# Values ahead of keys in the second layer's projections, samples' values from the same weights, and another spread of the projection units over the steps

## The reference

```python
def shared_kv(x, c, w_ada_kv, b_ada_kv, w_kv):
    sh, sc = jnp.split(c @ w_ada_kv + b_ada_kv, 2, axis=-1)
    kv = modulate(x, sh, sc) @ w_kv          # 1024 -> 1024 key columns, then 1024 value columns
    return kv[..., :KW_B].reshape(...), kv[..., KW_B:].reshape(...)
...
q = (xm @ w_q_b[lb]).reshape(n, t, H_B, 2 * DH_B) * (DH_B ** -0.5)
if prompt:
    o = diff_attn_prompt(q, k_sh, v_sh, lam)               # 512 x 512 scores, 8 heads x 2 maps
else:                                                      # 8 samples x 16 cached pages of 128 rows, and the own new row
    o = diff_attn_sample(q, k_sh, v_sh, cache_k, cache_v, page_table, lam)
```

## Time and profile before

| what | value |
|---|---|
| median of 3 runs | 1865.09 us (1860.26 to 1868.95) |
| the profiled execution's own time | 1866.28 us |
| its span, first to last instruction | 1864.4 us |
| PE busy in the span | 1551.1 us (83%) |
| DVE, ACT, POOL busy | 687.9, 404.3, 348.7 us |
| HBM read, written | 521.82 MB, 40.03 MB |

### The profile page before, as it was taken

The page is one execution under the profiler, slowest core; times in us unless marked ns, Lnnn a source line. Parts: engine busy times, 40 slices in busy tenths (PEclk is TensorE's granted clock), DMA queues, the critical chain, the costliest instruction groups (busy, mean ns, idle before and its releaser), DMA issues. The chain is left out here.

```text
span 1864.4 us, 21819 instructions
## 1 busy us (share of the span) xinstructions
PE 1551.1 (83%) x7246; PEld 675.7 (36%) x7247; DVE 687.9 (37%) x1228; ACT 404.3 (22%) x911; POOL 348.7 (19%) x277
## 2 busy tenths in 40 slices
PE   5899996597588999966999997777893699989964
PEld 2333344443333333323343333444442333333321
DVE  1001118575300000145954458997365200100007
ACT  1001015221121122212121113445221021312220
POOL 0000001000100000011735468783000100100001
PEclk8999997698799999977999997888896799999986
DMA  8564705726599999869879999999514499999953
GB/s 320 194 269 175 273 2 181 252 99 249 227 426 419 396 374 425 354 258 328 303 283 375 386 365 410 355 354 356 188 36 192 173 424 381 421 418 402 427 237 129
DMA packets 119420, 551.63 MB, mean 296 GB/s; under 512 B 16453, under 2 KB 37814, under 8 KB 97307
## 3 DMA queue, kind: packets, MB, share of 16 engines
q1 hardware_dynamic: 94962, 492.46, 67.0%
q10 hardware_dynamic: 15424, 37.28, 5.4%
q0 software_dynamic: 8944, 20.76, 3.1%
HBM read 521.82 MB, written 40.03 MB: 301 GB/s over the span
## 5 line engine op out<-in xcount | busy, mean ns | idle before, releaser
L1631 PE MATMUL ps<-arena_w,arena_r 128*64 128x512 f32 x1600 | 367.4, 616 | 27.2 <-issue 22.2
L1631 PEld LDWEIGHTS ps<-arena_w,arena_r 128*64 128x64 f32 x1600 | 120.6, 142 | 267.1 <-issue 261.0
L1613 PE MATMUL ps<-arena_w,arena_r 128*64 128x512 f32 x800 | 183.4, 606 | 19.3 <-ACT arena_r L1661 19.3
L1708 DVE TENSOR_TENSOR arena_r<-arena_r,ps 128x512 f32<-128x512 f32 x38 | 26.1, 688 | 422.8 <-ACT arena_r L1678 422.8
L2074 POOL TENSOR_TENSOR arena_w<-arena_w,arena_r 128x1024 f32<-128x1024 f32 x55 | 129.7, 2362 | 84.0 <-DMA arena_w<-in_cache_k_dram 83.6
L2074 POOL TENSOR_TENSOR arena_r<-arena_r 128x1024 f32<-128x1024 f32 x56 | 134.7, 2410 | 46.8 <-DMA arena_r<-in_cache_k_dram 46.4
L2127 PE MATMUL ps<-arena_w,xt 128*128 128x512 f32 x256 | 113.5, 600 | 1.3 <-ACT xt L2379 1.3
L451 PE MATMUL ps<-arena_w,xt 128*128 128x512 f32 x256 | 113.1, 597 | 1.0 <-DVE arena_w L534 0.6
L1562 POOL COPY small<-idx 128x1 int32 (+1 forms) x38 | 7.0, 183 | 510.8 <-PE ps L1579 459.6
L1613 PEld LDWEIGHTS ps<-arena_w,arena_r 128*64 128x64 f32 x800 | 55.5, 138 | 120.9 <-issue 99.0
L1677 ACT ACTIVATE arena_r<-ps 64x512 f32<-64x512 f32 x38 | 22.4, 590 | 342.1 <-PE ps L1631 342.1
(11 more groups left out here) (426 smaller groups left out, 1960.2 us busy)
## 6 DMA issues: line engine op xcount, KB each, us to landing
arena_w<-in_w_exp_gate_dram SPq DMA_DIRECT2D x38, 2048.0 KB, 10.5
arena_w<-in_w_exp_up_dram SPq DMA_DIRECT2D x38, 2048.0 KB, 19.0
arena_w<-in_w_exp_down_dram SPq DMA_DIRECT2D x38, 2048.0 KB, 17.0
arena_m<-in_cache_v_dram SPq DMA_DIRECT2D x120, 512.0 KB, 6.8
arena_w<-in_cache_k_dram SPq DMA_DIRECT2D x64, 512.0 KB, 7.2
arena_r<-in_cache_k_dram SPq DMA_DIRECT2D x64, 512.0 KB, 6.8
arena_w<-in_w_ada_dram SPq DMA_DIRECT2D x12, 2048.0 KB, 11.9
arena_m<-in_w_ada_dram SPq DMA_DIRECT2D x12, 2048.0 KB
```

Of the source, the lines that this page charges most:

```text
L1613: last = nc.tensor.matmul(psy[c][at:at + 64, :], ht[u][:, k, 64 * (1 - a):64 * (2 - a)], wd[u][:, k, c * 512:(c + 1) * 512], start=(k == 0 ...
L1631: last = nc.tensor.matmul(ps[at:at + 64, :], xgt[u][:, k, 64 * a:64 * (a + 1)], w[u][:, k, :], start=(k == 0), stop=(k == KT - 1), tile_po ...
```

## The change

- In the prompt's projections the two halves of `w_kv` change places: units 8 to 15 are now the values and 16 to 23 the keys. The stores of the prompt's keys and values change places with them.
- The samples' own value rows are no longer multiplied with weights of their own in M: `own_parts` of chunks 8 to 11 reads the pairs in `both` that the prompt's value units use. The four 1 MB loads on ACT's queue go. These pieces move from steps 1 to 5 into steps 5 to 7 (two `own_parts` in 5, two sums and two parts in 6, two sums in 7).
- ACT waits for these pieces (`sp_mm` at 10 and 12) before it loads the next pair into a buffer.
- Units per step: two in each of steps 1 to 4, from step 5 on four in three steps; before, three in two steps throughout.
- SP waits once, for 8 own pieces, where it waited for 10 and for 12. The first `vn` (sample 0) is issued in SP's step 10 instead of 8; the others stay.
- The store of the new value rows moves from ACT's step 5 to 7, and the one that SP reads back goes first. PE's first turning of keys waits for unit 19.

```diff
     def load_pair(self, eng, a, c):
-        src = a["w_kv"].rearrange("(p k) n -> p k n", k=KT)[:, :, (c - self.QCH) * self.CW:(c - self.QCH + 2) * self.CW]
+        half = self.QCH if c < 2 * self.QCH else -self.QCH
+        c0 = (c - self.QCH + half) * self.CW
+        src = a["w_kv"].rearrange("(p k) n -> p k n", k=KT)[:, :, c0:c0 + 2 * self.CW]
...
-        count = lambda g: 3 * g // 2
+        early = self.QCH
+        count = lambda g: 2 * g if g <= early else 2 * early + 4 * (g - early) // 3
...
+    OWN_V = 5
+    split = lambda g: {OWN_V: (2 * QCH, 2 * QCH + 1), OWN_V + 1: (2 * QCH + 2, 2 * QCH + 3)}.get(g, ())
+    summed = lambda g: split(g - 1)
...
-                if g in (LAG, LAG + 1):
-                    sp.wait_ge(sp_mm, NCH - 2 * (LAG + 1 - g))
+                if g == LAG:
+                    sp.wait_ge(sp_mm, 2 * QCH)
...
-                if g >= LAG and (g - LAG) % 4 == 2:
-                    b = (g - LAG) // 4
+                if g == LAG + 4 or g > LAG + 4 and (g - LAG) % 4 == 2:
+                    b = (g - LAG - 2) // 4
...
+                elif c < 2 * QCH:
+                    pe.wait_ge(mk_in[c % QCH], 16)
+                    w, x = own_w[c % QCH], xskv
                 else:
-                    pe.wait_ge(mk_in[c % QCH], 16 * (c // QCH))
-                    w, x = own_w[c % QCH], xskv
+                    pair, half = (c - 2 * QCH) // 2, c % 2
+                    pe.wait_ge(dec.w_in[2 * pair], 32)
+                    w, x = dec.both[pair][:, :, half * CW:(half + 1) * CW], xskv
...
-                if 1 <= g <= 5:
-                    if g >= 2:
-                        own_sum(2 * QCH + g - 2)
-                    if g <= QCH:
-                        own_parts(2 * QCH + g - 1)
+                for c in summed(g):
+                    own_sum(c)
+                for c in split(g):
+                    own_parts(c)
                 if g == FIRST - 1:
+                    pe.wait_ge(it_ev, item_of(5 * QCH - 1) + 1)
                     k_transpose(0)
...
-                if c < 2 * QCH:
-                    s.dma_start(own_w[c - QCH], dec.source(a, c + QCH)).then_inc(mk_in[c - QCH], 16)
...
                     if i == NQ - 1 and c + 4 < NCH:
+                        s.wait_ge(sp_mm, c + QCH + 2)
                         dec.load_pair(s, a, c + 4)
...
-                    if g == 5:
-                        s.wait_ge(ssa_ev, 2 * QCH)
-                        s.dma_start(a["v_sample"].rearrange("b s h d -> (b s) (h d)"), vrow).then_inc(nv_out, 16)
-                        s.dma_start(m.newD[1], vrow).then_inc(nv_out, 16)
+                if g == OWN_V + 2:
+                    s.wait_ge(ssa_ev, 2 * QCH)
+                    s.dma_start(m.newD[1], vrow).then_inc(nv_out, 16)
+                    s.dma_start(a["v_sample"].rearrange("b s h d -> (b s) (h d)"), vrow).then_inc(nv_out, 16)
```

More of the change, by code:

```diff
@@ L2390, in unit_out @@
                     c0 = (c - QCH) % QCH
-                    nc.scalar.copy((kk, vv)[c // QCH - 1][:, i, c0 * CW:(c0 + 2) * CW], bank[:, :]).then_inc(it_ev, 1)
+                    nc.scalar.copy((vv, kk)[c // QCH - 1][:, i, c0 * CW:(c0 + 2) * CW], bank[:, :]).then_inc(it_ev, 1)
                     if i == NQ - 1 and c + 4 < NCH:
+                        s.wait_ge(sp_mm, c + QCH + 2)
                         dec.load_pair(s, a, c + 4)
@@ L2397, in unit_out @@
                     s.wait_ge(it_ev, n + 1)
-                    name, t = (("k", kk), ("v", vv))[c // QCH - 1]
+                    name, t = (("v", vv), ("k", kk))[c // QCH - 1]
                     s.dma_start(a[f"{name}_prompt"].rearrange("b g p h d -> p (b g) (h d)"), t).then_inc(out, 16)
@@ L2487, in _ @@
                     unit_out(u)
[L2488 to L2492, removed]
-                    if g == 5:
-                        s.wait_ge(ssa_ev, 2 * QCH)
-                        s.dma_start(a["v_sample"].rearrange("b s h d -> (b s) (h d)"), vrow).then_inc(nv_out, 16)
-                        s.dma_start(m.newD[1], vrow).then_inc(nv_out, 16)
+                for c in summed(g):
+                    own_row(c)
+                for c in split(g):
+                    own_rows(c)
+                if g == OWN_V + 2:
+                    s.wait_ge(ssa_ev, 2 * QCH)
+                    s.dma_start(m.newD[1], vrow).then_inc(nv_out, 16)
+                    s.dma_start(a["v_sample"].rearrange("b s h d -> (b s) (h d)"), vrow).then_inc(nv_out, 16)
                 if g == FIRST - 1:
```

## The result

The changed kernel takes 1873.96 us (median of 20 runs, 1867.68 to 1881.58), the kernel before, on the same chip in the same rounds, 1864.40 us (20 runs): the ratio is 1.005, with a 95% interval of 1.0036 to 1.0064. It is slower by some 9.5 us; the forecast was no change, and 1873.96 lies above the range. The profiled execution after took 1871.72 us, with a span of 1869.0.

The account below looks back on a forecast made before the run. PE's chain was taken to bound the kernel up to step 17, DVE and pages behind it. -12.8 + 8.5 + 1.6 + 2.5 = -0.2 us on the profiled 1866.28 gave 1866.1, so 1865 us as median; range 1855 to 1872.

Parts of the forecast that it names:

- Parts 1 and 2: Own-value loads go, unit 0 starts 9.2 us sooner; two units a step; PE's lead 12.8 us after value group 0.
- Part 3: At the end of value group 3: `vn` takes 11 us behind queued pages, so PE stalls 8.5 us.
- Part 4: Behind the stall: slower work on PE, 1.6 us; in step 12 a wait for value group 6, 2.5 us.
- One for one behind step 17: Behind step 17, bound by DVE and pages: the rest shifts by as much as step 17 does.
- The stall outgrows the lead: Rival: `vn` takes 14 us or more, stall 11.5, step 12 waits 4.3; +4.6 us, 1870; chance 0.15.
- The lead lives: Rival: `vn` lands within 5 us of its issue, through a gap between pages; 1853 to 1857 us; chance 0.20.
- DVE and pages hold anyway: Rival: step 15's softmax waits for key pages, so step 17 stays where it was; 1863 to 1867 us; chance 0.13.
- The second pair: Rival: weights land late, own piece 10 waits in step 6, 0 to 3 us; 1865 to 1868; within the forecast's 0.52.

Follow-up runs that it names:

- no_own_loads: The kernel before without the four own-value weight loads on ACT's queue, new values projected with the key weights: 1863.28 us, ratio 0.9985 to before.
- spread_only: The kernel before with only the new spread of projection units over the steps: 1875.31 us, ratio 1.0038 to before.
- swap_only: The kernel before with only the halves of `w_kv` and their stores swapped: 1864.82 us, ratio 0.9990 to before.
- rhythm_store_row: The changed kernel with `vn` in SP's step 9, the prompt's value store in ACT's step 20, units pulled into steps 9, 12, 15: 1856.58 us, 0.9941 to before.
- before_again: The kernel before, unchanged, run once for a second profile: 1006.9 us from the load of the page table to the end.
- vn_step9: The changed kernel with the first `vn` issued in SP's step 9 instead of 10: 1862.25 us, ratio 0.9972 to before.

## Why the prediction was wrong

**Parts 1 and 2 held.** Unit 0 starts at 880.9 as forecast. Value group 0 ends at 965.8, 1.6 us before the forecast, with step 4 waiting 0.69 us for DVE where 1.5 was taken. PE's lead there is 8.0 + 7.1 - 0.6 = 14.5 us; 12.8 was forecast. no_own_loads and spread_only show that neither half gives it alone: by the same count they have no lead and one of 5.8 us when value group 0 is done.

**Part 3 held.** The stall is 7.80 us, with 0.92 ahead of it for the pages of group 3, 8.7 in all where 8.5 was forecast; the row took 10.3 us where 11 was taken. Its mechanism is shown twice, by moving `vn` one step ahead (no wait, 0.78%) and by giving it a queue without pages (5.7 us). The profiled execution after shows the same beside `vn` itself: 512 KB on POOL's queue, issued between 994 and 1001, landed in 7.0 us, where SP's pages of these microseconds took 12.0 to 12.4. The rule of the Trainium skill, "DMA: Bandwidth & Descriptors", section on queues, rings and completion order, that an engine of the DMA takes a queue's descriptors in ring order, agrees with the 10.3 us behind the pages and the 5.7 us without them.

**Part 4 is the step that failed**: 4.1 us were charged, the rows show about 19. Its first term, the slow clock behind the stall, was put at 1.6. It is (3.59 - 1.89) + (16.33 - 14.00) = 4.0: I priced the first small matmuls and not the two units behind them, although had 15.65 us for two units behind a wait of only 2.6. Its second term, step 12, was put at 2.5 and at most 4.3. It is the wait of 6.54 for group 6; then 2.67 for DVE, and slower matmuls again, 3.62 - 1.91, 0.61 - 0.39, 16.36 - 14.00 and 8.83 - 7.1, 6.0 in all; together 15.2 us.

The wait itself was mis-sized by 2 to 5 us. The last page of group 6 goes out at 1038.27, PE is ready at 1046.57, and it comes at 1053.11: a cover of 8.3 us and a latency of 14.8. I had a cover of 9.4 and took latencies of 11.3 to 13.7 from the earlier trace rows. The prediction reads the earlier trace rows as group 7's pages; they are group 8's. Group 7's, issued right behind the pair and the store (issues 1036 to 1045), landed sooner:

```profile
arena_m<-in_cache_v_dram SPq DMA_DIRECT2D x4, 512.0 KB, 11.0
```

So no row that the sum used had a latency of 14.8. The rest was not in the sum at all: that a second stop brings its own wait for DVE and its own slow clock.

With these the account closes: -14.5 + 8.7 + 4.0 + 15.2 = +13.4 at step 17, where +12.9 is read.

**One for one behind step 17** is not borne out either. From there to the end of the span after takes 1869.0 - 1117.67 = 751.3 us where before took 756.4 and 754.2, so of 12.9 us late 8 to 10 are left. That the stretch has slack for a lateness is not shown by this: swap_only, not 2 us late at step 17, takes 1858.9 - 1107.98 = 750.9 us too. That it takes back some of a lead, the 768.2 us of rhythm_store_row show; all other runs take 747 to 758.

**The rivals.** "The stall outgrows the lead" named the right sign and the wrong place: the stall is as forecast, and step 12 and the clock carry the loss. "The lead lives" is refuted by the wait for `vn`, and "DVE and pages hold anyway" by the late step 17 and by rhythm_store_row, which begins it 15.7 us sooner; no_own_loads alone came out as that rival expected. The second pair held nothing up.

**The single edits.** By their times the parts of the loss do not add up: the wait for `vn` is worth 14 us, the changed kernel without it is still 5 us faster than before with step 12's stop in it, and the spread with that same stop but without the other edits is 7 us slower. At step 17 they do. From the load of the page table to the end of value group 10, and from there to the end of the span, the profiled executions took:

| kernel | load of the page table at | to the end of group 10 | from there to the end |
|---|---|---|---|
| before, before_again | 857.55, 853.97 | 250.4, 252.8 | 756.4, 754.2 |
| after | 854.08 | 263.6 | 751.3 |
| vn_step9 | 855.00 | 252.8 | 747.7 |
| spread_only | 857.35 | 260.1 | 750.7 |

The rows of vn_step9 and of spread_only that end group 10:

```profile
1105.91 1.91 PE L2153 MATMUL ps<-arena_m,arena_r 128*16 128x512 f32 x16
```
```profile
1115.57 1.91 PE L2143 MATMUL ps<-arena_m,arena_r 128*16 128x512 f32 x16
```

Without the wait for `vn` the lead of 14.5 and the 15.2 of step 12 cancel: +0.7, where 0 to 2.4 is read. spread_only has the same stop and a lead of only 5.8: +9.4, where 9.7 is read beside the first before. What stays open lies behind step 17: the 5 us by which vn_step9 is faster than before are no lead at step 17, and no experiment takes that stretch apart.

## What to carry to other kernels

A small load that an engine needs soon belongs ahead of the large loads on its queue, or on a queue without them; moving it by one step of the loop was worth 0.78% here, more than the whole loss. When work is spread anew, count for each step what PE has to do beside the loads of that step: PE did not wait for the pages beside the pair and the store when it had two units to do, and stopped when it had one. Charge a stop of a full PE with the slow matmuls behind it, here 4 to 6 us for stops of 8 to 9, and look for the next wait in what else has become late.

## What the runs showed of the hardware

The wait for DVE in step 12 has an odd cause. DVE's and POOL's rows there, and the same DVE instruction in step 8:

```profile
980.07 0.22 DVE L2636 TENSOR_SCALAR small<-ident,small 16x16 f32<-16x16 f32 x1
...
1056.98 2.36 DVE L2636 TENSOR_SCALAR small<-ident,small 16x16 f32<-16x16 f32 x1
```
```profile
1056.97 2.34 POOL L2081 TENSOR_TENSOR arena_r<-arena_r 128x1024 f32<-128x1024 f32 x1 [2.75 <-DMA arena_r<-in_cache_k_dram]
```

A 16x16 instruction that takes 0.22 us alone took 2.36, as long as the multiplication of a key page that POOL began 0.01 us earlier, and ended with it. The Trainium skill, "SBUF — State Buffer", section on the two separate sides, says that VectorE and GpSimd share a pair of ports by an exclusive lock that the first holder keeps for its whole instruction. The rows agree with that; which form of the instruction asks for the lock, no run here shows.
